# One group of small attention products per unit between the tiles of a projection, instead of two

## The reference

```python
proj = jnp.einsum('bld,dc->blc', rmsnorm_2(h, attn_norm_g), w_in)
fq, fk, fv, flog, rq, rk, rv, rg = jnp.split(proj, SPLIT_POINTS, axis=-1)
# fox attention, 8 heads of 64; c = cumsum(log_sigmoid(flog + b))
s = einsum('bhqd,bhkd->bhqk', q, k) * scale + c_q[..., :, None] - c_k[..., None, :]
p = softmax(where(k_pos <= q_pos, s, -inf));  out = einsum('bhqk,bhkd->bhqd', p, v)
# retention, 4 heads of 128: rotated q and k, decayed scores, group norm, silu(rg)
```

## Time and profile before

| | us |
|---|---|
| median of 3 runs | 3584.01 |
| lowest and highest | 3582.62, 3591.16 |
| the profiled execution, its own time | 3596.02 |
| its span, from first to last instruction | 3594.2 |
| TensorE busy with matmuls | 3279.3 |
| VectorE busy | 1811.7 |
| ScalarE busy | 1127.9 |
| GpSimd busy | 260.6 |

### The profile page before, as it was taken

One profiled execution on the slowest core, in us unless ns is written; L12 is line 12 of the kernel. 1 busy time (PEld: TensorE's weight loads), 2 busy tenths in 40 slices (PEclk: granted clock), 3 DMA queues, 4 the chain that ended last, 5 costly groups with the idle time before them and its releaser, 6 DMA issues. The chain is left out here.

```text
span 3594.2 us, 52412 instructions
## 1 busy us (share of the span) xinstructions
PE 3279.3 (91%) x20898; PEld 2872.0 (80%) x20898; DVE 1811.7 (50%) x2677; ACT 1127.9 (31%) x1675; POOL 260.6 (7%) x214
## 2 busy tenths in 40 slices
PE   1999986999998899888999599999999899899997
PEld 1668775888887668766888598789999897799997
DVE  8547578544544647554333424554344434544343
ACT  2243223222222343223333343233222432233222
POOL 2000101011011000110111200010000100010001
PEclk9999888999999899889999799999999999999999
DMA  6101013322323201012222111112222211122322
GB/s 245 59 5 63 26 73 115 118 105 102 120 105 120 97 1 67 26 47 82 94 93 93 66 42 48 48 65 92 95 94 88 83 42 42 48 89 81 105 83 88
DMA packets 79087, 283.38 MB, mean 79 GB/s; under 512 B 10584, under 2 KB 10712, under 8 KB 77280
## 3 DMA queue, kind: packets, MB, share of 16 engines
q1 hardware_dynamic: 74912, 264.48, 20.9%
q0 software_dynamic: 3168, 11.31, 0.8%
q10 hardware_dynamic: 864, 5.57, 0.4%
HBM read 279.20 MB, written 2.10 MB: 78 GB/s over the span
## 5 line engine op out<-in xcount | busy, mean ns | idle before, releaser
L311 PE MATMUL ps<-h_hi,hi_ring 128*128 128x264 f32 (+2 forms) x4208 | 1343.9, 319 | 84.6 <-DVE h_lo L601 42.4
L311 PE MATMUL ps<-h_lo,hi_ring 128*128 128x264 f32 (+2 forms) x4208 | 1313.0, 312 | 0.0
L311 PE MATMUL ps<-h_hi,lo_ring 128*128 128x264 f32 (+2 forms) x4208 | 1310.8, 312 | 0.0
L311 PEld LDWEIGHTS ps<-h_hi,hi_ring 128*128 128x128 f32 (+1 forms) x4208 | 796.7, 189 | 167.7 <-issue 94.1
L311 PEld LDWEIGHTS ps<-h_lo,hi_ring 128*128 128x128 f32 (+1 forms) x4208 | 798.1, 190 | 50.8 <-issue 3.2
L311 PEld LDWEIGHTS ps<-h_hi,lo_ring 128*128 128x128 f32 (+1 forms) x4208 | 794.3, 189 | 47.1
L240 DVE TENSOR_TENSOR lo_ring<-ring,hi_ring 128x1024 fp32r<-128x1024 f32 (+1 forms) x414 | 490.1, 1184 | 645.4 <-ACT hi_ring L230 641.5
L230 ACT ACTIVATE hi_ring<-ring 128x1024 fp32r<-128x1024 f32 (+1 forms) x414 | 425.0, 1026 | 1226.0 <-PE ps L311 1204.7
L311 PE MATMUL ps<-hid_hi,hi_ring 128*128 128x512 f32 (+1 forms) x1472 | 474.5, 322 | 3.0 <-DVE hid_lo L839 2.7
L311 PE MATMUL ps<-hid_lo,hi_ring 128*128 128x512 f32 (+1 forms) x1472 | 475.3, 323 | 0.0
L311 PE MATMUL ps<-hid_hi,lo_ring 128*128 128x512 f32 (+1 forms) x1472 | 475.3, 323 | 0.0
(11 more groups left out here) (279 smaller groups left out, 3168.6 us busy)
## 6 DMA issues: line engine op xcount, KB each, us to landing
ring<-weights_dram SPq DMA_DIRECT2D x350, 512.0 KB, 3.2
mod_ring<-w_mod_dram SPq DMA_DIRECT2D x64, 512.0 KB, 4.1
ring<-weights_dram SPq DMA_DIRECT2D x64, 384.0 KB, 2.9
arena<-w_mod_dram SPq DMA_DIRECT2D x32, 512.0 KB, 3.5
x<-x_dram SPq DMA_DIRECT2D x1, 3072.0 KB, 16.3
arena<-c_rows_dram ACTq DMA_DIRECT2D x3, 1024.0 KB, 7.3
arena<-ret_decay_dram POOLq DMA_DIRECT2D x2, 1056.0 KB, 7.1
silu_rows<-c_rows_dram ACTq DMA_DIRECT2D x2, 1024.0 KB, 5.2
```

The source lines that it names most:

```text
L311: ins = nc.tensor.matmul(out[0:m, c:c + n], w, a[:, t0:t0 + n], start=first and k == 0 and p == 0, stop=last and k == kts - 1 and p == 2)
```

## The change

The three small products of a unit's turn are issued in one group at the head of each half block: `weigh(u - 2)`, `scores(u)`, `turn(u - 1)`. All of a unit's `turn` and `weigh` thus come one step later in the queue than before, and four tiles follow one group without interruption. ScalarE and VectorE queues are reordered to match, and the waits that guard the area are restated.

```diff
-    weighed_by = lambda j, s: min(max(slot_unit(j, s), 0), n_units)
+    turned_by = lambda j: min(max(slot_unit(j, 1), 0), n_units)
+    weighed_by = lambda j: min(max(slot_unit(j, 1) - 1, 0), n_units)
...
-            def weigh(u):
+            def weigh(u, blocks_done):
                 n, r = rows(u), real(u)
                 pe.wait_ge(turned_in.sem, turned_in.at(u + 1))
+                area_free(0, blocks_done, 0)
... (turn_block)
-                area_free(weighed_by(j + 1, 1), n, sums_done)
+                if turned_by(j + 1):
+                    pe.wait_ge(turned_in.sem, turned_in.at(turned_by(j + 1)))
+                area_free(weighed_by(j + 1), n, sums_done)
... (TensorE, tile loop)
-                    if k % 4 == 0 and is_unit(u):
-                        scores(u)
+                    if k % 4 == 0:
+                        if is_unit(u - 2):
+                            weigh(u - 2, blocks_done)
+                        if is_unit(u):
+                            scores(u)
+                        if is_unit(u - 1):
+                            turn(u - 1, blocks_done)
                     last = tile_product(nc, core.buf(j), w, k, KT, acts, SEQ2)
...
-                    if k % 4 == 0 and is_unit(u - 1):
-                        weigh(u - 1)
...
-                    if k % 4 == 3 and is_unit(u):
-                        turn(u, blocks_done + (s == 1 and j - 1 in to_turn))
... (ScalarE)
+                if is_unit(u - 1):
+                    copy_probs(u - 1)
+                if is_unit(u + 1):
+                    exponents(u + 1)
                 if is_unit(u):
                     copy_probs(u)
-                if is_unit(u + 1):
-                    exponents(u + 1)
-                    copy_probs(u + 1)
... (VectorE)
+                if is_unit(u - 2):
+                    finish(u - 2)
                 if is_unit(u):
                     peak_of(u)
-                if is_unit(u - 1):
-                    finish(u - 1)
-                if is_unit(u):
                     invert(u)
...
+                if j in SCORE_SLOTS:
+                    weight_scores(SCORE_SLOTS.index(j))
+                if is_unit(u - 1):
+                    finish(u - 1)
                 if is_unit(u + 1):
                     peak_of(u + 1)
-                if is_unit(u):
-                    finish(u)
-                if j in SCORE_SLOTS:
-                    weight_scores(SCORE_SLOTS.index(j))
```

## The result

The changed kernel takes 3615.22 us (median of 7 runs, 3611.61 to 3645.55) against 3587.64 for the kernel before in the same series. The ratio is 1.0097, 95% interval 1.0076 to 1.0118: 27.6 us slower by the medians, 35 (27 to 42) by the ratio. The forecast was 21.4 us of slowdown and a time of 3605, in a range of its own from 3597 to 3613. The sign and the places were right; the size was not, and what was missing is the clock.

The account below looks back on a forecast made before the run. TensorE was taken as the bound, busy 98.00 of 98.00 us in the attention units' stage. Per layer 7.4 + 3.9 + 1.6 - 1.4 - 0.8 = 10.7, for two 21.4 us slower: 3605 us median, own range 3597 to 3613.

Parts of the forecast that it names:

- TensorE's own stream: Entries into tiles behind small groups: one fewer per unit, 0.03 us gained each, 0.8 us per layer.
- The copy of the odd unit: `weigh(u - 1)` at k = 4 waits for ScalarE's late copy of its transposes: 7.4 us lost per layer.
- `turn` for `finish`: `turn(u)` at k = 4 waits for VectorE's `finish(u - 1)` in blocks 14, 15, 18: 3.9 us lost per layer.
- `turn_block`: Behind k = 5 it waits for `copy_probs(u)` in blocks 7, 10, 13, 16, 17: 1.6 us lost per layer.
- Block 19: Small products move into TensorE's existing 2.33 us wait for VectorE's weighted scores: 1.4 us gained per layer.
- The sum at full clock: All holes less the gains over the attention units' stage: 10.7 us slower per layer, 21.4 for two.
- The clock: Attention stage: holes stay below 2 us, where the trace showed no clock loss, so nothing was added.
- The rival: Clock falls behind the larger holes (blocks 9, 11, 14, 17, 18): +16 us, 3621 us, chance 0.12.

Follow-up runs that it names:

- the best version: Changed kernel with ScalarE's copies moved earlier (last unit's excepted) and VectorE's `finish` ahead of `part_lo`: 3588.25 us, ratio 0.9988 to the kernel before.
- the kernel before with holes: Kernel before, two groups per unit, with ScalarE copying odd units' transposes three or four times so TensorE waits ahead of `weigh`: 3632.6 us, ratio 1.0111.

## Why the prediction was right in its places and wrong in its size

- **TensorE's own stream** (0.8 us per layer, bounds 0 and 5.3). Inside the bounds, on the low side. If block 19 gains the forecast 1.4, the best version's 2.4 us per layer and its hole of 0.8 leave about 1.8 for the entries, 0.06 each instead of 0.03. This is an estimate, it splits what I did not measure apart.
- **The copy of the odd unit** (7.4 us). Right. TensorE's 24 distances into `weigh` sum to 10.1 us, against 0.13 each without a hole: 7.0. Block 9 was forecast at 1.36 and is 1.37, block 17 at 1.6 and is 2219.83 - 2218.17 - 0.12 = 1.54.
- **`turn` for `finish`** (3.9 us). Right: 1.5 in block 14 (forecast 1.55), 1.9 in block 18 (1.9), about 0.3 in block 15 (0.45).
- **`turn_block`** (1.6 us). Right: in layer 2 four distances of 0.30 to 0.54 instead of 0.12, and one of 0.55 in block 17, 1.6 in all.
- **Block 19** (gain of 1.4). Right in kind: the wait fell from 2.33 to 0.53 us, where the prediction had about 0.8; a wait of `turn(27)`, 0.5 us, is new and was not foreseen.
- **The sum at full clock** (10.7 us per layer). Measured 9.1, the 201.2 us of above against 192.1. The three kinds of holes are 7.0 + 3.7 + 1.6 = 12.3 us, so block 19 and the stream gave back 3.2, where the forecast had 2.2. Each term is a little off to the same side.
- **The clock: this step failed.** The prediction put it: "The holes here stay below 2 us, where this trace shows none of it". I took one lone hole of 1.66 us, in the earlier trace rows, as proof for some ten holes of 0.7 to 1.9 us in a row, and put the clock at zero in the sum and at 0.12 among the rivals. It is what is measured above the holes and the stream: 27.6 us (medians) or 35 (ratio) less 18, so 9 to 17 us, and 8 and 20 in the two profiled executions (their stages, 410.2 and 421.9 us, less 2 x 201.2). The rival's price, 16 us, lies in that range, and its 3621 us was the nearer number. The clock alone does not make up the distance from 3605 to 3615.22: the sum was 3 us too high for both layers, and the kernel before has 3587.64 in this series, 3.6 above the 3584.01 that the sum was added to. By the rule of the Trainium skill, TensorE: Matmul & The Clock Gate, section "A second HAM failure mode: psum-queue depth-cycling", the holes were to cost more than their length; the runs agree, with 10.2 us of clock beside 10.2 us of holes in the kernel before with holes. The section gives no length of such an idle; here holes of up to 0.6 us left the clock full, and those of 0.4 to 1.3 us did not.

## What to carry to other kernels

When a consumer is moved in one engine's queue, write down for each place that it now waits both paths from their common start; the sum of the waits was right here to 0.6 us per layer, 12.9 forecast and 12.3 measured. Count the whole queue behind a moved instruction too: putting the late copy ahead of `part_hi` removed 7 us of waits per layer and gave 6 of them back two engines on. And in a program that TensorE fills, price repeated holes of 1 us and more at up to twice their length for the clock, and those of half a microsecond at their length; a single such hole elsewhere says nothing on either.

## What the runs showed of the hardware

- Eleven holes of 0.4 to 1.3 us between block 4 and block 17, between stretches in which TensorE is full, took the granted clock from 1.00 to 0.87 in one stretch of 50 us and to 0.93 in another. Holes of up to 0.6 us at the same places left it at 1.00.
- A lone wait can take it down too, and need not: the 23 us around the wait of 2.33 us in block 19 of the kernel before have a clock of 0.93 in layer 2 and of 1.00 in layer 1.
- Where holes made it fall, the loss differs between executions and layers of one program: the changed kernel's stage took 205.6, 204.6, 214.2 and 207.7 us in four passes over the same holes, against 201.2 at full clock. In the kernel before with holes it was equal in both layers, 215.49 and 215.48 us.
- One more group of wide transposes between the tiles costs 0.01 us (three groups against two).
